# Conditioning panels of five turns on VectorE, a crossed order of the first two weight units behind each norm, and a tile-wise pass into the second block

## What is computed

```python
m = (s_c @ ada_w[i] + ada_b[i]).reshape(B, N_MOD, 1, D)
x = half_step_ffn(x, m[:, 0], m[:, 1], m[:, 2], ...)          # norm 0 (layer 0), norm 3 (layer 1)
x = post_norm_update(x, y_lat, m[:, 5], 1.0, ...)             # norm 1, norm 4
x = half_step_ffn(x, m[:, 6], m[:, 7], m[:, 8], ...)          # norm 2, norm 5; norm 5 feeds the second block
```

## Time and profile before

| | before |
|---|---|
| median of 3 runs | 3013.8 us |
| the profiled execution | 3014.72 us |
| its span in the profile | 3012.9 us |
| TensorE clock granted, mean | 0.99 |

### The profile page before, as it was taken

One profiled execution on the slowest core, in us unless ns is written; L12 is line 12 of the kernel. 1 busy time (PEld: TensorE's weight loads), 2 busy tenths in 40 slices (PEclk: granted clock), 3 DMA queues, 4 the chain that ended last, 5 costly groups with the idle time before them and its releaser, 6 DMA issues. The chain is left out here.

```text
span 3012.9 us, 51229 instructions
## 1 busy us (share of the span) xinstructions
PE 2898.0 (96%) x19396; PEld 2540.7 (84%) x19396; DVE 1765.8 (59%) x2644; ACT 1356.7 (45%) x1928; POOL 375.3 (12%) x306
## 2 busy tenths in 40 slices
PE   6999999899999999999899999999999999999998
PEld 3667765677888889888899989899999998988998
DVE  2323224267766667666545866757855577566784
ACT  1222213125655544554344544455644454436563
POOL 2111100113110110211100120201101002020110
PEclk8999999999999999999999999999999999999999
DMA  9986354751565655465435505245555451533564
GB/s 325 285 252 195 103 164 130 198 168 49 158 184 154 194 183 160 148 195 182 142 120 167 161 28 176 92 134 153 170 162 161 137 154 57 160 114 112 161 179 135
DMA packets 586157, 474.79 MB, mean 158 GB/s; under 512 B 28721, under 2 KB 547889, under 8 KB 585665
## 3 DMA queue, kind: packets, MB, share of 16 engines
q1 hardware_dynamic: 584464, 460.44, 49.8%
q0 software_dynamic: 1520, 11.95, 1.3%
HBM read 471.23 MB, written 4.72 MB: 158 GB/s over the span
## 5 line engine op out<-in xcount | busy, mean ns | idle before, releaser
L2309 DVE TENSOR_TENSOR low<-raw,high 128x1024 fp32r<-128x1024 f32 (+1 forms) x744 | 904.6, 1219 | 801.0 <-ACT high L2079 798.6
L2079 ACT CAST high<-raw 128x1024 fp32r<-128x1024 f32 (+1 forms) x744 | 768.1, 1034 | 987.9 <-PE PS L1987 604.7
L1985 PE MATMUL PS<-NHh,high 128*128 128x272 f32 (+1 forms) x2304 | 669.0, 290 | 11.4 <-DVE NHl L1752 6.9
L1987 PE MATMUL PS<-NHh,low 128*128 128x272 f32 (+1 forms) x2304 | 660.8, 287 | 0.0
L1986 PE MATMUL PS<-NHl,high 128*128 128x272 f32 (+1 forms) x2304 | 660.0, 286 | 0.0
L1985 PEld LDWEIGHTS PS<-NHh,high 128*128 128x128 f32 x2304 | 433.3, 188 | 16.9 <-issue 9.1
L1986 PEld LDWEIGHTS PS<-NHl,high 128*128 128x128 f32 x2304 | 433.9, 188 | 0.8
L1987 PEld LDWEIGHTS PS<-NHh,low 128*128 128x128 f32 x2304 | 433.6, 188 | 0.0
L1983 PE MATMUL PS<-XX,high 128*128 128x512 f32 x966 | 347.8, 399 | 0.0
L1985 PE MATMUL PS<-XX,high 128*128 128x512 f32 (+1 forms) x752 | 273.5, 364 | 6.9 <-DVE XX L2370 4.4
L1982 PE MATMUL PS<-XX,low 128*128 128x256 f32 x966 | 272.4, 282 | 1.4 <-DVE XX L2370 1.0
(11 more groups left out here) (351 smaller groups left out, 4868.7 us busy)
## 6 DMA issues: line engine op xcount, KB each, us to landing
raw<-w_in_dram SPq DMA_DIRECT2D x416, 256.0 KB, 3.0
raw<-ffn_w_in_dram SPq DMA_DIRECT2D x352, 256.0 KB, 3.4
part<-ada_w_dram SPq DMA_DIRECT2D x184, 256.0 KB, 4.2
raw<-w_ffn_in_dram SPq DMA_DIRECT2D x176, 256.0 KB, 3.2
raw<-ffn_w_out_dram SPq DMA_DIRECT2D x160, 256.0 KB, 3.1
raw<-w_branch_dram SPq DMA_DIRECT2D x96, 256.0 KB, 3.0
raw<-w_ffn_out_dram SPq DMA_DIRECT2D x80, 256.0 KB, 3.0
part_sg<-ada_w_dram SPq DMA_DIRECT2D x48, 256.0 KB, 3.0
```

The source lines that it names most:

```text
L1985: nc.tensor.matmul(out, wh, xh, start=begin, stop=False)
L1987: last = nc.tensor.matmul(out, wl, xh, start=False, stop=end)
L2079: nc.scalar.copy(high[:, slot, 0:nk, :], raw[:, slot, 0:nk, :]).then_inc(s_high, 1)
L2309: nc.vector.tensor_tensor(low[:, slot, 0:nk, :], raw[:, slot, 0:nk, :], high[:, slot, 0:nk, :].bitcast(F32), ALU.subtract).then_inc(s_low, 1)
```

## The change

1. **Hosts and buffers.** Turns 1 and 2: 32 parts in groups of four behind chunks 2, 4, ..., 16. Turns 3 to 7 (80 parts): one by one behind chunks 18 to 28, 30 to 40, 46 to 54, 56 to 64, 66 to 74. Turn 8: pairs behind 76 to 83. 16 part buffers in place of 9, and a part is loaded behind the load of chunk host + 8 of its buffer's last user (before: host + 4).
2. **Turns 3 to 7 on DVE.** After the `low` of chunk host + 4, `ada_accumulate` does two DVE instructions a part, each on [128, 512]. The four accumulators are then summed over the partitions by four PE matmuls with a column of ones (`ada_sum`), two chunks after the last host (`sum_after`), into the bank that `ada_rows` reads.
3. **Crossed order.** In `steps[0]`, `glu`, `v`, `cgate` and the steps behind an rms norm, the first four chunks are (unit 0, chunk 0), (1, 0), (0, 1), (1, 1), and in unit 0 j runs inside k. Unit 0 is complete one chunk later (`finished`). Rolled loops start at their second round.
4. **Start.** The second unit's first chunk is loaded with the first's, before panel 1; panel 3 is multiplied behind the first chunk; 9 and 5 warming matmuls (`keep_warm`) stand before panels 2 and 1; `x_low` goes by pairs.
5. **Into the second block.** Behind norm 5 DVE scales tile by tile with `g` and 1/sigma in one instruction, ACT squares each tile with `b` as its bias (into `TQ`), and DVE adds `b` into `H` beside that. ACT no longer writes `H`; the wait for the constants moves behind the squares.

```diff
-ADA_HOSTS = ((0, 32, 80), (44, 24, 24), (68, 16, 24))
+ADA_HOSTS = ((2, 16, 32, 4), (18, 11, 16, 1), (30, 11, 16, 1), (46, 9, 16, 1), (56, 9, 16, 1), (66, 9, 16, 1),
+             (76, 8, 16, 2))
+ON_DVE = range(3, 8)
...
-    return [S0 + x * n // parts for S0, n, parts in ADA_HOSTS for x in range(parts)]
+    return [S0 + x // group * group * n // parts for S0, n, parts, group in ADA_HOSTS for x in range(parts)]
...
+        def part_room(S):
+            if S < 44:
+                return range(6) if S < 32 else (0, 1, 3, 4) if S < 36 else (0, 3)
+            return ROWS if S < 68 else (TAIL, *TOP)
...
-            due = HOST[before] + 4 if before is not None else {PSG: 47, PRS: 47, TAIL: 71}.get(part_slot[A], 1)
+            first = 3 + max(0, A - 1) if HOST[A] < 44 else 52 + (HOST[A] - 46) if HOST[A] < 68 else 75
+            due = HOST[before] + 8 if before is not None else first
...
+            late = s["crossed"] and isinstance(u, int) and u == 0
+            return s["S0"] + len(s["kch"]) * (u + 1) + 4 + late
...
+                elif slot in TOP:
+                    sp.wait_ge(s_res, KT + 4)
...
+            def load_crossed(s):
+                for c, (k0, nk) in enumerate(s["kch"]):
+                    for u in range(2):
+                        S = s["S0"] + 2 * c + u
+                        if S >= NSLOT:
+                            sp.wait_ge(s_low, S + 1)
+                        if S > 1:
+                            load(raw[:, 2 * c + u], s_raw[2 * c + u], s["src"](u, k0, nk))
+                        for A in issued_after(S):
+                            load_part(A)
...
+            def ada_sum(t):
+                pe.wait_ge(s_adak, parts_done(4 * TURN * t - 1, True))
+                pe.wait_ge(s_adarow, t - 1)
+                for x in range(TURN):
+                    last = nc.tensor.matmul(PS[32 * x:32 * x + 32, ROW_BANK + t % 2, :],
+                                            ONEW[:, 2 * (TURN - x) - 1:2 * (TURN - x) + 31], ada_acc(t, x),
+                                            start=True, stop=True)
...
+                        order = [(j, k) for j in range(2) for k in range(nk)]
+                        if first_rows:
+                            order = [(j, k) for k in range(nk) for j in range(2)]
...
+                if s["crossed"]:
+                    for c in range(2):
+                        for u in range(2):
+                            gemm_unit(u, u, s["S0"], 0, c)
+                            if s is steps[0] and (u, c) == (0, 0):
+                                for q in range(4):
+                                    ada_part(3, q)
...
+            def ada_accumulate(A):
+                t, x, c = turn_of(A), A // 4 % TURN, A % 4
+                slot = part_slot[A]
+                dve.wait_ge(s_part[slot], 32 * part_slot[:A + 1].count(slot))
...
+                for y in range(2):
+                    k = 2 * c + y
+                    src, acc = flat(parts_at[slot][:, 2 * y:2 * y + 2, :]), ada_acc(t, x)
+                    if k == 0:
+                        ins = nc.vector.tensor_scalar(acc, src, silu[:, k:k + 1], None, ALU.mult)
+                    else:
+                        ins = nc.vector.scalar_tensor_tensor(acc, src, silu[:, k:k + 1], acc, ALU.mult, ALU.add)
...
+                dve.wait_ge(s_adak, parts_done(A, True))
...
-                        act.wait_ge(s_res, 6 * KT + KT)
-                        act.wait_ge(s_meta, 32)
-                        for v in range(4):
-                            rms_act_pair(act, 0, v, None)
+                        act.wait_ge(s_meta, 16)
+                        nc.scalar.activation(TQ[:, :, 0:N_META], H[:, :, 0:N_META], ACT.Square)
+                        for k in range(KT):
+                            act.wait_ge(s_modd, KT * 6 + k + 1)
+                            ins = nc.scalar.activation(TQ[:, k, N_META:T2], TC[:, k, 0:T], ACT.Square,
+                                                       bias=sm("xb")[:, k:k + 1])
...
-                        standardise(0)
-                        standardise(1).then_inc(s_modd, 1)
+                        for k in range(KT):
+                            nc.vector.scalar_tensor_tensor(TC[:, k, 0:T], TC[:, k, 0:T], sm("xg")[:, k:k + 1],
+                                                           RS[:, 1, 0:T], ALU.mult, ALU.mult).then_inc(s_modd, 1)
+                        for k in range(KT):
+                            dve.wait_ge(s_modd, KT * 6 + k + 1)
+                            nc.vector.tensor_scalar(H[:, k, N_META:T2], TC[:, k, 0:T], sm("xb")[:, k:k + 1], None,
+                                                    ALU.add).then_inc(s_res, 1)
```

More of the change, by code:

```diff
@@ L494, in behind, with finished @@
                     two(i)
+        for s in steps:
+            name = s["name"]
+            s["crossed"] = s is steps[0] or name in ("glu", "v", "cgate") or bool(s.get("after_rms"))
+        def finished(s, u):
+            late = s["crossed"] and isinstance(u, int) and u == 0
+            return s["S0"] + len(s["kch"]) * (u + 1) + 4 + late
         def unit_of(S):
@@ L1817, in _ @@
                 else:
-                    for u in range(s["units"]):
+                    for u in range(2 if s["crossed"] else 0, s["units"]):
                         load_unit(s, u, u % 2, s["S0"] + nch * u)
@@ L1950, in rows_ready, with gemm_unit @@
                         pe.wait_ge(s_hl, s["hid0"] + 2 * c)
-                def gemm_unit(u, p, S, slot0):
+                def gemm_unit(u, p, S, slot0, only=None):
                     kch = s["kch"]
                     for c, (k0, nk) in enumerate(kch):
-                        pe.wait_ge(s_low, S + c + 5)
+                        if only is not None and c != only:
+                            continue
+                        first_rows = isinstance(u, int) and u == 0 and s["crossed"]
+                        at = S + c if only is None else s["S0"] + 2 * c + u
+                        pe.wait_ge(s_low, at + 5)
                         rows_ready(u, c, k0 + nk)
@@ L1988, in gemm_unit @@
-                        last.then_inc(s_chunk, 1)
-                        for A in ada_parts(S + c):
-                            ada_part(ADA_FIRST + A // 4, A % 4)
+                            if name in ("glu", "v", "cgate") and (first_rows if s["crossed"] else rolled(s) or not u) and j == 0:
+                                pe.wait_ge(s_xl, KT * norms + k0 + k + 1)
+                            if s.get("after_rms") and (first_rows if s["crossed"] else rolled(s) or not u) and j == 0 and k % 2 == 0:
+                                pe.wait_ge(s_rxl, 4 * (rmss - 1) + (k0 + k) // 2 + 1)
@@ new lines, in gemm_unit @@
+                            wh = high[:, slot, k, j * P:(j + 1) * P]
+                            wl = low[:, slot, k, j * P:(j + 1) * P]
+                            xh, xl = mh[:, k0 + k, t0:T], ml[:, k0 + k, t0:T]
+                            begin, end = k0 + k == 0, c == len(kch) - 1 and k == nk - 1
+                            if wide(s, u):
+                                two = bank(p, j).rearrange("p a (x n) -> p (a x) n", x=2)
+                                both = (XX if mh is XH else GG)[:, :, k0 + k, 0:T]
+                                if begin:
+                                    nc.tensor.matmul(two, wh, both, start=True, stop=False)
+                                    last = nc.tensor.matmul(out, wl, xh, start=False, stop=False)
+                                else:
+                                    nc.tensor.matmul(out, wl, xh, start=False, stop=False)
+                                    last = nc.tensor.matmul(two, wh, both, start=False, stop=end)
+                                continue
@@ new lines, in gemm_unit @@
+                            nc.tensor.matmul(out, wh, xh, start=begin, stop=False)
+                            nc.tensor.matmul(out, wh, xl, start=False, stop=False)
+                            last = nc.tensor.matmul(out, wl, xh, start=False, stop=end)
+                        last.then_inc(s_chunk, 1)
+                        for A in ada_parts(at):
+                            if turn_of(A) not in ON_DVE:
+                                ada_part(ADA_FIRST + A // 4, A % 4)
+                        if isinstance(S, int) and S + c in sum_after:
+                            ada_sum(sum_after[S + c])
@@ L2003, in _ @@
                 U_end, nch = s["U0"] + s["units"], len(s["kch"])
+                if s.get("norm") and norms == 0:
+                    pe.wait_ge(s_ones, 1)
+                if s["crossed"]:
+                    for c in range(2):
+                        for u in range(2):
+                            gemm_unit(u, u, s["S0"], 0, c)
+                            if s is steps[0] and (u, c) == (0, 0):
+                                for q in range(4):
+                                    ada_part(3, q)
                 if rolled(s):
-                    with pe.Fori(0, s["units"] // 2) as i:
```

(8 more changed lines are left out.)

149 lines of the change are left out of this document (89 added, 60 removed).

## The result

The changed kernel takes 2948.6 us in the median of four runs (2942.8 to 2954.0), the kernel before 3015.7 in the median of four (3013.3 to 3019.8): ratio 0.9772, 95% interval 0.9755 to 0.9789. So 67 us are gained, 72 between the two profiled executions (3014.7 and 2942.8), where 93 were forecast. The time lies above the range of 2905 to 2942.

A forecast was written before the change was run, and what follows sets the result against it. PE, busy 96% of the span, was taken as the bound. Gains of 61.7, 16.0, 10, 8.6 and 2.5 less 2.1, 1.7 and 2.0 make 93.0 us off 3014.7; less 0.9, 2921 us (8 in 10: 2905 to 2942).

The forecast's parts named there:

- Part 2: At host 44 and the hosts in `v`, PE's 10.9 us of waits for parts and 5.1 of clock go: gain 16.0 us.
- Part 7: At the start, first product at about 34 to 35 us, chunk 2 at about 52.5: gain 2.5 us (-1 to 6).
- Rival A: Late part loads on DVE, few buffers from hosts 36 and 68 on, hand waits to PE: +20, 2941 us; chance 0.17.
- Part 1: PE's visits to conditioning parts between chunks fall from 91.3 to 29.6 us: gain 61.7 us (55 to 63).
- Part 3: DVE's own work on 80 parts, 128 us, is hidden by PE's work: priced at 0, up to 15 us.
- Part 4: What gets in the way around norm 0, in `v` and at turn 8: costs of 2.1, 1.7 and 2.0 us.
- (a): Before norm 0's centring, host 67's two parts and turn 6's row copy stand on DVE: +2.1 us (0 to 4).
- (b, c): In `v`, unit 0's copy comes late, +1.7 us (0 to 6); turn 8 has three buffers, +2 us (0 to 8).
- Part 5: Crossed order behind norms 0 to 4 and four rms norms shortens PE's waits for tiles: gain 10 us (2 to 14).
- Part 6: Behind norm 5, into the second block, the first rms scaling comes sooner: gain 8.6 us (6 to 9.5).

The follow-up runs named there:

- run 13: The kernel before the change with the `rpb_skew` store and bias loads moved as in run 5: 3011.6 us, against 3013.2 on the same chip, ratio 0.9987.
- run 1: Changed kernel with all twelve bias loads moved from `v` behind the third rotation of `k`, their masks to the end of `q`: 2938.2 us.
- run 2: Changed kernel with POOL's store of `rpb_skew` moved from 61.6 us to behind unit 20 of the first step: 2939.2 us.
- run 7: run 5 with turn 6 on hosts 56 to 63 and turn 7's first four parts on hosts 65 and 66: 2921.4 us.
- run 12: run 7 with all turns multiplied by TensorE (`ON_DVE` empty): 3009.6 us.
- run 11: run 7 with one more VectorE instruction (accumulator times 1.0) behind each of the 160 instructions on parts: 2953.9 us.
- run 5: Changed kernel with the store moved as in run 2, bias loads in threes groups behind `k`'s first three rotations, masks in `q`'s first units: 2930.8 us.
- run 6: Changed kernel with the crossed order taken back everywhere but in the first step: 2954.6 us.
- run 8: Changed kernel with the pass into the second block taken back, ScalarE writing whole rows of `H` and then squaring pairs: 2953.9 us.
- run 10: Changed kernel with the twelve bias loads on SP's hardware queue, behind raw loads 77, 79 and 81, in place of POOL's software queue: 2948.7 us.
- run 3: Changed kernel with the store late and the bias table cut beforehand, loaded in `v` in 6 transfers of pieces up to 1536 bytes: 2935.0 us.

## Why the prediction was wrong, part by part

**Part 2 is the step that failed.** It took 10.9 us of waits for parts and 5.1 of clock as a property of the hosts, and let them go with the re-hosting: "gain 16.0 us". 8.1 of the 10.9 stood in `v` and right behind its last chunk, and they were the bias loads' (run 13). The change leaves these loads where they are, so the waits stay; only their place changes, from TensorE to VectorE, and VectorE's order hands them on with interest: the copy of a value unit at 511.0 us, 12.6 later than in run 1 (498.4), a wait of TensorE for it and one for a part of turn 8, and 10 us at half clock. 17 us lost by the bias loads (run 1), where a gain of 12 had been booked. The number in the earlier trace rows was right; that it was not asked whose DMA filled those microseconds was the mistake. Only the wait at host 44 (2.5 and 1.7 of clock) went as forecast.

**Part 7, the start.** The first product at 33.79 and chunk 2 at 52.88 were forecast (34 to 35, 52.5). What failed is that nothing was priced between chunk 2 and 6. Host 4 takes four parts in one visit, and the store, which in the kernel before cost 0.8 us there (run 13), holds up the raw loads in front of the last two: 9.3 us (run 2), where part 7 and the visits together had booked a gain of 7.7 by chunk 6. That is rival A's mechanism on TensorE.

**Rival A** named the mechanism (a late load, VectorE's order, TensorE waits) and "from 68 on" as a place. It put the cause in reuse of buffers, spread over 80 parts. It was one cause at two places, 26 us together in their own stretches (runs 1 and 2). At 0.17 it had too little chance.

**Part 1** was too small. The gaps were read rightly; what I left out is that the chunk behind a visit is slower too. From its first product to its last it takes 5.35 us (5.39 behind three or four parts) and 5.21 with no visit before it, and 0.11 of the difference is the first product, 0.34 us from the next and not 0.23. So a visit of one or two parts costs 1.22 us and not 1.07 to 1.09 (chunks 24 to 29 take 32.64 us without visits in run 7 and 39.95 with six in run 12), one of three 2.11, one of four 2.12 and a sum 1.22. Before that makes 16 x 2.11 + 56 x 1.22 = 102.1 us, after 8 x 2.12 + 13 x 1.22 = 32.8: about 69 us and not 61.7, and most of the 6.6 us by which the hosts' stretch was better. The Trainium skill (TensorEngine Tiling (Array Packing), Tiling Modes) says that a change of tiling mode drains TensorE; a part's matmuls use 32 columns of the array and products 128, and the slow first product agrees with it.

**Part 3** held where it mattered: up to 371 us no chunk is longer even with the added work (run 11). The second step has little room left. The durations came out at 0.75 and 0.48 us, 1.54 a part. The rule of the Trainium skill that it weighed (SBUF — State Buffer, Who interferes with whom) agrees with the trace. 13 of the 160 accumulations took 1.5 to 1.8 us, each of them one that began within a GpSimd subtraction or addition (11 with two inputs in SBUF, and two `tensor_scalar`, which have one). One of them in the timeline (the pair took 2.57 where others take 1.54):

```profile
227.34 1.55 POOL L2845 TENSOR_TENSOR GG<-SG,GG 128x512 fp32r<-128x512 f32 x1 [9.33 <-ACT GG L2301]
227.66 2.57 DVE L2435 SCALAR_TENSOR_TENSOR adarow<-part,silu,adarow 128x512 f32<-128x512 f32 x2
```

**Part 4.** (a) 4.8 us and not 2.1: both parts and the copy fell on the path whole (3.1 + 0.7), and the gap before the second sum brought half clock; run 7 takes 2.6 back, against run 5. (b, c) With the bias loads away `v` and `k` take 108.1 us together (run 1: 46.0 and 62.1), where 107.3 had been forecast. So the late copy and turn 8's buffers together cost about what was said; their shares were not tried.

**Part 5** was 10: the undoing gives 12.3, of which `k` takes 3.0 back (run 6). **Part 6** was 8.6: the two traces give 8.4, the undoing 7.0 (run 8), with part of the sum at a higher clock than before. Signs, places and sizes stand, but for `v`, where the crossing gained nothing behind the late copy.

The table closes the sum: 93.0, less 9.7 at the start, 17.9 in `v` and `k`, 2.7 at norm 0 and 0.2 at norm 5, plus 6.6 in the hosts' stretch, 1.2 and 1.5 behind: 71.8, but for rounding. The two transfers alone are 26 of what was lost (runs 1 and 2); that visits were dearer than priced hid part of the miss, and that was luck.

## What to carry to other kernels

A wait for a DMA names the buffer, not the cause. Before a change is credited with its end, list what every queue moves in those microseconds, and ask whether the change moves that. When a wait is moved from the engine that bounds the kernel to one with slack, look at what stands behind it in that engine's order: an epilogue that frees a bank hands the wait straight back. And a transfer needed much later (a table, a store) belongs where no just-in-time load runs; here moving two of them, and two parts off a norm, was worth 27 us (2921.4 against 2948.6), more than a third of what the whole change brought.

## What the runs showed of the hardware

- Beside the software queue the hardware queue falls far back. Between 64 and 72 us (store) it moved almost nothing, between 484 and 502 us 0.1 to 0.4 MB in most 2 us, where it moves 0.7 alone. Page, part 3 (queue: packets, MB, share):

```profile
q1 hardware_dynamic: 584464, 460.44, 50.8%
q0 software_dynamic: 1520, 11.95, 1.3%
```

  That is 7.9 kB in the mean of the software queue against 0.8 kB, but the mean mixes two sizes. The trace's packet records have the store as 64 packets of 57 kB (2.5 to 3 us each) and the bias loads as 768 of 4.1 kB, beside packets of 1 and 2 kB of SP's queue. The Trainium skill (DMA: Bandwidth & Descriptors, Queues, rings and completion order) says that each DMA engine takes turns between queues by whole packets. If what the trace counts is what the page calls a packet, which no run shows, the trace agrees: from 496 to 500 us the software queue had 200 packets and the hardware queue 254, almost one for one, with 0.69 MB against 0.28. Run 10 sent the same bytes through SP's queue in 12288 packets of 256 bytes and `v` and `k` were no shorter, so the turns are not the whole cost.
- Small pieces cost in the hardware queue as well: 183 GB/s at full share in run 10, against 321 in the same place without them (run 1). On the software queue 1536-byte pieces landed no faster (run 3); the packets there were nearly as large as before (4.6 and 4.1 kB).
- Half clock comes and goes in stages that no edit touches. Window 1875 to 1890 us of run 2 and of run 7:

```profile
1875.00:1890.00 15.00, 13.28 (x68) 11.68 (x67) 7.84 (x41) 7.51 (x30) 0.00 (x0) 0.66 0.12 37
```

```profile
1875.00:1890.00 15.00, 15.00 (x107) 13.51 (x107) 7.23 (x10) 11.18 (x18) 0.00 (x0) 1.00 0.22 71
```

  That is 4.3 us in one place, and it is why gains were read from stretches and not from medians.
